# Branch products in three passes, and GpSimd making the low weight parts of the mixing loop

## The reference

```python
for l in range(DEPTH):                      # 2 layers
    x = x + 0.5 * swiglu(rms_norm(x, norm_g[l, 0]), ffn...)
    h = rms_norm(x, norm_g[l, 1])
    qa, ..., vc = split(h @ w_in[l])
    ya = neighbourhood_attention(qa, ka, va, na_rpb[l])     # 8 heads, width 512
    yb = diff_attention(qd, kd, vd, ...)                    # 4 heads, normed, width 512
    yc = window_gqa(qc, kc, vc, ...)                        # 8 heads, width 512
    g = sigmoid(h @ w_gate[l] + b_gate[l])                  # 3 x 1024
    merged = (g[:, :, 0] * (ya @ w_branch[l, 0]) + g[:, :, 1] * (yb @ w_branch[l, 1])
              + g[:, :, 2] * (yc @ w_branch[l, 2]))         # w_branch: 3 x 512 x 1024
    x = x + merged @ w_o[l]
    x = x + 0.5 * swiglu(rms_norm(x, norm_g[l, 2]), ffn...)
```

## Time and profile before

| | |
|---|---|
| median of 3 runs | 1992.77 us |
| the profiled execution | 1993.51 us, of which its span 1991.7 |
| PE | busy 1940.5 us, 97% of the span |
| DVE | 1223.4 us, 61% |
| ACT | 703.2 us, 35% |
| POOL | 0.2 us |
| mean granted TensorE clock | 0.994 |
| mixing loop, layer 0 and 1 | 301 to 447.7 us, 948 to 1094 us |

### The profile page before, as it was taken

How to read it: one execution, slowest core, us unless ns; L and a number is a source line. 1 busy time by engine, 2 the same in 40 slices (tenths; PEclk the granted TensorE clock), 3 DMA queues, 4 the chain that set the end, 5 groups by cost and what they waited for, 6 DMA issues and landing times.

```text
span 1991.7 us, 33632 instructions
## 1 busy us (share of the span) xinstructions
PE 1940.5 (97%) x14053; PEld 1598.8 (80%) x14053; DVE 1223.4 (61%) x2117; ACT 703.2 (35%) x1052; POOL 0.2 (0%) x4
## 2 busy tenths in 40 slices
PE   9999999999999999999999999999898999999997
PEld 9999998889999999999888999999665444434432
DVE  6665759877567877775987777757766333222221
ACT  5433536535334543353653534343332000000001
POOL 0000000000000000000000000000000000000000
PEclk9999999999999999999999999999899999999999
DMA  7798563276776677656325675654309999999996
GB/s 238 240 346 267 174 189 117 96 204 207 224 221 203 212 233 228 200 182 185 117 96 180 206 239 185 197 121 128 127 22 340 421 421 421 421 422 421 421 421 280
DMA packets 275282, 476.66 MB, mean 239 GB/s; under 512 B 29254, under 2 KB 235136, under 8 KB 250552
## 3 DMA queue, kind: packets, MB, share of 16 engines
q1 hardware_dynamic: 274876, 474.38, 68.9%
q10 hardware_dynamic: 252, 0.08, 0.0%
HBM read 473.27 MB, written 7.95 MB: 242 GB/s over the span
## 4 chain that ended last, share of the span: by engine, by line
PE 82%; DMA 11%; DVE 5%; ACT 1%; SPq 1%; issue 1%; DVEq 0%; ACTq 0%
PE ps L780 80%; DMA ring_over<-in_moe_w_up_dram 4%; DMA ring_zone<-in_moe_w_up_dram 3%; DMA hl_place<-in_moe_w_gate_dram 1%; DMA hl_place<-in_moe_w_up_dram 1%; DMA hT<-in_moe_w_up_dram 1%; SPq L700 1%; PE ps L1120 1%; PE ps L1263 0%; DVE PT L2353 0%; DVE WL L1978 0%; PE ps L1440 0%; DVE hl L1918 0%; ACT mT L1758 0%; ACT gT L1706 0%
## 5 line engine op out<-in xcount | busy, mean ns | idle before, releaser
L780 PE MATMUL ps<-hh,WH 128*128 128x256 f32 x2232 | 633.1, 284 | 1.3 <-DVE WL L1907 0.7
L780 PE MATMUL ps<-hl,WH 128*128 128x256 f32 x2232 | 622.9, 279 | 0.0
L780 PE MATMUL ps<-hh,WL 128*128 128x256 f32 x2232 | 622.9, 279 | 0.0
L1907 DVE TENSOR_TENSOR WL<-W,WH 128x1024 fp32r<-128x1024 f32 x390 | 471.6, 1223 | 244.0 <-ACT WH L1522 242.4
L1522 ACT ACTIVATE WH<-W 128x1024 fp32r<-128x1024 f32 x390 | 408.2, 1055 | 434.1 <-PE ps L780 398.2
L780 PEld LDWEIGHTS ps<-hh,WH 128*128 128x128 f32 x2232 | 418.8, 188 | 14.8 <-issue 11.6
L780 PEld LDWEIGHTS ps<-hl,WH 128*128 128x128 f32 x2232 | 418.7, 188 | 1.2 <-issue 1.0
L780 PEld LDWEIGHTS ps<-hh,WL 128*128 128x128 f32 x2232 | 418.8, 188 | 0.0
L780 PE MATMUL ps<-hid_h,WH 128*128 128x256 f32 x704 | 200.6, 285 | 0.0
L780 PE MATMUL ps<-hid_l,WH 128*128 128x256 f32 x704 | 197.6, 281 | 0.0
L780 PE MATMUL ps<-hid_h,WL 128*128 128x256 f32 x704 | 197.3, 280 | 0.0
(11 more groups left out here) (401 smaller groups left out, 2601.8 us busy)
## 6 DMA issues: line engine op xcount, KB each, us to landing
W<-in_ffn_w_gate_dram SPq DMA_DIRECT2D x88, 512.0 KB, 5.2
W<-in_ffn_w_up_dram SPq DMA_DIRECT2D x88, 512.0 KB, 4.8
W<-in_ffn_w_down_dram SPq DMA_DIRECT2D x88, 512.0 KB, 3.9
W<-in_w_in_dram SPq DMA_DIRECT2D x78, 512.0 KB, 4.6
...
W<-in_w_gate_dram SPq DMA_DIRECT2D x48, 512.0 KB, 4.5
```

What stands on the lines that cost most here:

```text
L780: ins = nc.tensor.matmul(o, lhsT, rhs, start=start, stop=stop, skip_group_check=True, **kw)
L1907: v.tensor_tensor(low, W[:, i % RAW, :], high.bitcast(F32), ALU.subtract).then_inc(low_ready, 1)
```

## The change

`w_branch` joins `SPLIT`. Its product becomes three passes, and so the head outputs are needed as high and low: new names `y_high` and `y_low` for 12 tiles each, laid over `yT` and over tiles of `QK` that are free by then. DVE writes both straight from PSUM for the first and third branch, and for the second copies and subtracts after the norm. One norm vector moves from `QK` tile 5 to tile 8. GpSimd makes every low part from the first `w_gate` piece to the last `w_branch` piece of a layer, 36 a layer; DVE skips them and goes on with `w_o`. The steps at which `w_o` is cast and subtracted follow from the common rule in place of `MIX_HALVES` and `MIX_RESTS`. SP waits for tile 15 (`merge_ready` 24l + 16) before it loads `w_ada` over `QK`. A pair used by two tiles is given back after the second, and the gate piece between with it.

```diff
-SPLIT = ("ffn_gate", "ffn_up", "ffn_down", "w_in", "w_gate", "w_in2", "w_o")
+SPLIT = ("ffn_gate", "ffn_up", "ffn_down", "w_in", "w_gate", "w_branch", "w_in2", "w_o")
...
+        _, QK_r, yT_r = zone(("before_QK", [P, TT * 1152], F32), ("QK_r", [P, 22, T], FR), ("yT_r", [P, 12, T], FR))
+        y_high = (*(yT_r[:, k, :] for k in range(4)), *(QK_r[:, 12 + k, :] for k in range(4)), *(yT_r[:, 8 + k, :] for k in range(4)))
+        y_low = (*(QK_r[:, 4 + k, :] for k in range(4)), *(yT_r[:, 4 + k, :] for k in range(4)), *(QK_r[:, 16 + k, :] for k in range(4)))
...
@@ SP, load_ada
                         sp.wait_ge(yn_ready, 4 * (l + 1))
+                        sp.wait_ge(merge_ready, 24 * l + 16)
...
@@ PE, mixing loop
-                        done_pair()
+                        if merged_tile(s) is not None and merged_tile(s) % 2 == 1:
+                            held["gates"] += 1
+                        else:
+                            done_pair()
...
-                            mm(ps[:, MERGE_BANK + j % 2, 0:T],
-                               chunk["b"][:, k * 256 + (i % 2) * P:k * 256 + (i % 2 + 1) * P],
-                               yT[:, branch * 4 + k, :], k == 0, k == 3, then=merge_ready if k == 3 else None)
+                            mm3(ps[:, MERGE_BANK + j % 2, 0:T], at(chunk["b"], k * 256 + (i % 2) * P),
+                                (y_high[branch * 4 + k], y_low[branch * 4 + k]), k == 0, k == 3,
+                                then=merge_ready if k == 3 else None)
                         if i % 2 == 1:
-                            done_plain()
+                            done_pair(1 + held["gates"])
+                            held["gates"] = 0
...
@@ ACT and DVE, mixing loop
+                    j = merged_tile(s)
+                    used((s < 24) + (j is not None and j % 2 == 0))
...
-                    if s in MIX_HALVES:
-                        used(1, ahead=0)
...
-                used(2, ahead=0)
+                used(4, ahead=0)
...
@@ DVE, rests
+                    if split_by_pool(n):
+                        st["split"] += 1
+                        continue
+                    if n and split_by_pool(n - 1):
+                        dve.wait_ge(low_ready, n)
...
@@ DVE, head values
-                        v.tensor_copy(yT[:, u // 2, :], ps[:, PV_BANK, 0:T]).then_inc(pv_free, 1)
+                        if u // 8 == 1:
+                            v.tensor_copy(yT[:, u // 2, :], ps[:, PV_BANK, 0:T]).then_inc(pv_free, 1)
+                        else:
+                            link(v.tensor_copy(y_high[u // 2], ps[:, PV_BANK, 0:T]))
+                            v.tensor_tensor(y_low[u // 2], ps[:, PV_BANK, 0:T], y_high[u // 2].bitcast(F32), ALU.subtract)\
+                                .then_inc(pv_free, 1)
...
@@ DVE, step 20, after the four scalings of yT
+                        link(ins)
+                        for h in range(4):
+                            ins = v.tensor_copy(y_high[4 + h], yT[:, 4 + h, :])
+                        link(ins)
+                        for h in range(4):
+                            v.tensor_tensor(y_low[4 + h], yT[:, 4 + h, :], y_high[4 + h].bitcast(F32), ALU.subtract)\
+                                .then_inc(yn_ready, 1)
...
@@ GpSimd
-            pass
+            for l in range(DEPTH):
+                pool.wait_ge(low_ready, pool_first[l])
+                for n in range(pool_first[l], pool_last[l] + 1):
+                    pool.wait_ge(high_ready, n + 1)
+                    high, low, _ = split_place(n)
+                    nc.gpsimd.tensor_tensor(low, W[:, split_at[n] % RAW, :], high.bitcast(F32), ALU.subtract)\
+                        .then_inc(low_ready, 1)
```

More of the change, by code:

```diff
@@ L554, in build, with split_by_pool @@
         plain_no = {i: n for n, i in enumerate(i for i in range(len(plan)) if i not in split_no)}
+        pool_first = [split_no[plan.index(("w_gate", l, 0, 0))] for l in range(DEPTH)]
+        pool_last = [split_no[plan.index(("w_branch", l, 11, 0))] for l in range(DEPTH)]
+        def split_by_pool(n):
+            return any(pool_first[l] <= n <= pool_last[l] for l in range(DEPTH))
         in2_at = split_no[plan.index(("w_in2", 0, CHUNK[ORDER[0]], 0))]
@@ L1070, in head_values @@
                                k == 0, k == 1, then=pv_ready if k and e else None)
+                held = {"gates": 0}
                 for s in range(MIX_STEPS):
@@ L1135, in _ @@
                         for h in range(4):
-                            mm(ps[:, SPREAD_BANKS[h], 0:T], ones[h * 32:h * 32 + 1, :], QK[h * 32:h * 32 + 1, 5, :],
+                            mm(ps[:, SPREAD_BANKS[h], 0:T], ones[h * 32:h * 32 + 1, :], QK[h * 32:h * 32 + 1, 8, :],
                                True, True, then=dn_spread)
@@ L1686, in _ @@
                 for s in range(MIX_STEPS):
+                    j = merged_tile(s)
+                    used((s < 24) + (j is not None and j % 2 == 0))
                     if s < 24:
                         b = s % 4
-                        used(1)
                         act.wait_ge(smax, due(smax))
@@ L1717, in _ @@
                         act.wait_ge(dn_sums, due(dn_sums))
-                        nc.scalar.activation(QK[:, 5, :], ps[:, PV_BANK, 0:T], ACT.Sqrt, bias=eps[:, :],
+                        nc.scalar.activation(QK[:, 8, :], ps[:, PV_BANK, 0:T], ACT.Sqrt, bias=eps[:, :],
                                              scale=1.0 / P).then_inc(dn_root, 1)
-                    if s in MIX_HALVES:
-                        used(1, ahead=0)
-                    j = merged_tile(s)
                     if j is not None and j >= 16:
@@ L2292, in _ @@
                             dve.wait_ge(dn_spread, due(dn_spread))
[L2293 to L2295 removed]
+                            ins = v.scalar_tensor_tensor(out=yT[:, 4 + h, :], in0=yT[:, 4 + h, :],
+                                                         scalar=subg[:, l:l + 1], in1=ps[:, SPREAD_BANKS[h], 0:T],
+                                                         op0=ALU.mult, op1=ALU.mult)
+                        link(ins)
[5 more added lines that the diff above has]
+                                .then_inc(yn_ready, 1)
                     if s < 24:
@@ L2324, in _ @@
                             link(v.tensor_scalar(g, g, 0.5, 0.5, ALU.mult, ALU.add))
-                    if s in MIX_RESTS:
-                        used(1, ahead=0)
                 mixed_low(KD - 1)
-                used(2, ahead=0)
+                used(4, ahead=0)
                 update_mixed(1.0, lambda k: col("norm_g", l * 24 + 16 + k))
```

7 lines of the change are left out of this document (1 added, 6 removed).

## The result

The changed kernel takes **2064.82 us** (median of 4 runs, 2063.10 to 2067.52) against 1992.77 for the kernel before on the same chip (median of 3; a fourth run, at 2879 us, was disturbed and is left out): a ratio of 1.0363, interval 1.0351 to 1.0376. The forecast was 2025, range 1985 to 2052. The direction and the mechanism were right, the size was not: +32 forecast, +72 measured.

What follows compares the result with a forecast made beforehand. PE was taken as the bound (82% of the span), with DVE within 0.2 us a pair of steps. Terms -14.9 + 3.4 + 12.7 + 22.8 + 8.4 = +32.4 us gave a median of 2025 us, range 1985 to 2052.

Steps and rivals of the forecast that it cites:

- The lock: In the mixing loop, certain DVE instructions must wait for a whole running GpSimd low part: +22.8 and +8.4 us.
- the chain of the prediction: Steps 0 to 11: `nm` waits for GpSimd's low part, +1.2 and +1.45 us; DVE's pair 10.85 us against PE's 8.95.
- the sign: Expected in traces, steps 0 to 11: `nm` starts over 1 us late; PE's idle time is put down to DVE's scores read.
- D: Length of one GpSimd low part of 1024 columns, taken as 2.0 us; bounded below by 1.22, above by 7.0.
- The term of 22.8: Steps 0 to 11, both layers: DVE waiting for GpSimd makes each of 6 pairs 1.9 us longer, +22.8 us.
- Steps 12 to 23: Three low parts fall into PE's longer pair; DVE is 0.3 to 1.5 us over, 0.7 taken: +8.4 us.
- Head norm +3.4 us: Step 20: four added casts and subtractions on DVE make tile 8 1.7 us late, +3.4 us for two layers.
- End of loop +12.7 us: Tail: `w_o` loads behind `w_ada`, so its casts and subtractions come late; PE waits 6.35 us a layer.
- Three passes -14.9 us: Each `w_branch` tile takes 1.42 us as 12 passes, 0.31 less than before; 24 tiles in each of 2 layers.
- Edits at no price: Other moved work, such as ACT's added casts and buffer waits, taken as hidden while DVE isn't late.
- The held pairs: ACT's casts wait for buffer pairs PE still uses, delaying exponentials; hidden, or up to 1 us a pair if DVE is late.

Runs made afterwards that it cites:

- `tiny_gpsimd`: The changed kernel with GpSimd subtracting only 2 of the 1024 columns of each low part, same waits and order: 2006.3 us.
- experiment 5: GpSimd makes only the `w_gate` low parts in the kernel before: 2018.9 us; changed kernel with `w_gate` low parts whole, `w_branch` ones 2 columns: 2047.5 us.
- `tiny_mended`: `tiny_gpsimd` with squares first in step 18, ACT's casts behind the exponentials in steps 12 to 23, `w_ada` loads behind `w_o`: 1994.0 us.

## Why the prediction was wrong, point by point

Per layer, the loop's stretches give it: forecast +11.4 and +4.8, measured +12.7 and +21.7 in layer 0, +12.7 and +24.9 in layer 1. Nearly all of the miss is behind step 12.

- **The lock, and on small instructions too: right.** `nm` was the main victim, as the chain of the prediction had it. The inverse sums, which it had too, weren't held (164 ns). And the sign was another than the prediction gave: `nm` starts on time and its record is longer, and PE's waits in these steps are mostly put down to ACT's copies of the transposes (0.5 and 1.5 us), not to DVE's reading of the scores.
- **D, the length of a GpSimd low part: 2.0 forecast, 2.39 measured**, nearer the estimate of 2.25 from the Trainium skill's figure (GPSIMD Engine Reference, Elementwise — side-by-side cycle accounting) than mine. By the prediction's own chain this would have made 2.7 us a pair in steps 0 to 11; the measured pair is 11.3 against 8.95, so 2.3, and the stretch 12.7 for 11.4. The term of 22.8 came out at 25, or at 27 against `tiny_gpsimd`.
- **Steps 12 to 23, "the same chain gives DVE 0.3 to 1.5 us over, I take 0.7" (+8.4 us): the step that failed.** The lock there costs 15.0 us in layer 0 and 19.3 in layer 1, 34 in all (`tiny_gpsimd` against the changed kernel). I had looked at `nm`, the inverse sums and the probabilities of a pair with DVE otherwise free. The lock lengthens DVE's records by 25.2 us a layer there, and not the records of those three alone: it also hits the four subtractions of the head norm (954 ns, not 420) and the sums `mT` (726, not 425). DVE's lateness then comes out in turn at each place that needs it: squares 5.12, norm 5.16, transposes 1.54 and 4.01. The prediction summed the lock and the change's other delays as if they were independent. They aren't: in the kernel before, 13.0 us of lock behind step 12 cost 0.5 us (experiment 5).
- **Head norm +3.4 us: right by itself, wrong beside the lock.** With 2 columns the wait is 1.55 us (1.7 forecast); in the changed kernel it is 5.16. The 3.6 us between count as the lock's.
- **End of loop +12.7 us: right.** 6.0 us of waiting a layer (in layer 0 5.99 changed, 6.05 with 2 columns; in layer 1 5.5 and 4.8) against 6.35; in the changed kernel's layer 0 2.81 of it stand before tile 20 and 1.65 before tile 22 (forecast 3.5 and 2.1); the cast started 7.5 us after tile 15 and not 6.4, the cycle was 4.7 us (4.8). That GpSimd costs nothing in the tail was wrong in kind (it delays `mT` to 2.31 us there), not in size.
- **Three passes -14.9 us: the price is right, the yield is not.** From the first scores of the loop to the first `w_o` product, less PE's waits, it is 147.5 us before and 140.9 in `tiny_mended`, so 6.6 us a layer and not 7.45. The gap is in the tail: 11 tiles take 18.9 us before and 16.1 there without the waits, 0.25 a tile saved and not 0.31.
- **Edits at no price.** The squares of step 18 stood 0.05 us ahead of PE. I never looked, since a limit that is just met shows as no wait. They and the transposes behind them cost 4.1 us a layer in `tiny_gpsimd`. The held pairs, which I priced at up to 1 us a pair, cost at most 3 us in all.
- **The clock: not in the sum at all.** The stretch from step 12 less its waits is 90.3 us in the changed kernel at a granted 0.94, 86.8 with 2 columns at 0.97, 85.2 in `tiny_mended` at 1.00; in layer 1 it is 93.1 at 0.90, 86.7 and 85.1. That is 5 us in layer 0 and 8 in layer 1, 13 in all (of which the lock's 34 hold 10), and they come on top of the waits, because PE runs at 1.2 GHz for a while after a long one. The difference was read from rows, not tested by an experiment of its own.

So, over both layers of the profiled executions: 27 + 34 for the lock, 11 for the tail, 3 for the norm, 8 for squares and transposes, -13 for the passes, 3 for the clock outside the lock. That is 73, against 72.2; what the lock adds to norm, squares, transposes and clock lies within its 34.
